# A two-layer hybrid transformer step: the loads of the first expert pairs, the last residual additions and the way of the outputs

## What is computed

```python
def layer(x, mod, P, l, ctx=None):
    h = rms_norm(x, P["norm_attn_pre"][l]) * (1 + sc1) + sh1
    a, new_ctx = token_mix(h, P, l, ctx)            # attention in three branches, gates, output projection
    x = x + g1 * rms_norm(a, P["norm_attn_post"][l])
    h = rms_norm(x, P["norm_ffn_pre"][l]) * (1 + sc2) + sh2
    x = x + g2 * rms_norm(moe(h, P, l), P["norm_ffn_post"][l])
    return x, new_ctx
```

## Time and profile before

| | us |
|---|---|
| median of 3 runs | 1754.84 (1752.04 to 1755.06) |
| the profiled execution | 1753.79 |
| its span, first to last instruction | 1752.0 |
| PE busy | 1679.8 (96%) |
| PEld, DVE, ACT, POOL busy | 900.7, 431.1, 321.6, 120.0 |
| share of PE in the chain that ended last | 91% |
| share of DMA in that chain | 4% |
| granted TensorE clock, mean | 0.986 of 2.4 GHz |
| moved by DMA | 559.88 MB |

### The profile page before, as it was taken

The page is one execution under the profiler, slowest core; times in us unless marked ns, Lnnn a source line. Parts: engine busy times, 40 slices in busy tenths (PEclk is TensorE's granted clock), DMA queues, the critical chain, the costliest instruction groups (busy, mean ns, idle before and its releaser), DMA issues.

```text
span 1752.0 us, 20948 instructions
## 1 busy us (share of the span) xinstructions
PE 1679.8 (96%) x8091; PEld 900.7 (51%) x8091; DVE 431.1 (25%) x1178; ACT 321.6 (18%) x754; POOL 120.0 (7%) x161
## 2 busy tenths in 40 slices
PE   4999998989999999999989999999899999999996
PEld 3878787643333333333367878784333333333332
DVE  1115443351111111111131444433311111111112
ACT  1010341021111111111120113302111111111111
POOL 3001000020000000001010000001100000000000
PEclk9999998999999999999999999899999999999998
DMA  9994232397999999999999633236879999999991
GB/s 354 418 388 161 88 105 70 139 363 302 367 424 426 426 424 425 425 426 425 418 394 404 226 109 105 85 108 253 341 288 414 426 425 425 425 423 425 426 426 80
DMA packets 60781, 559.88 MB, mean 320 GB/s; under 512 B 12972, under 2 KB 13120, under 8 KB 20240
## 3 DMA queue, kind: packets, MB, share of 16 engines
q1 hardware_dynamic: 45504, 528.50, 73.6%
q0 software_dynamic: 15184, 30.07, 5.0%
HBM read 576.02 MB, written 4.78 MB: 332 GB/s over the span
## 4 chain that ended last, share of the span: by engine, by line
PE 91%; DMA 4%; DVE 3%; issue 1%; ACT 1%; SPq 0%; POOL 0%; POOLq 0%; DVEq 0%; ACTq 0%; PEldq 0%
PE PS L1081 25%; PE PS L637 14%; PE PS L1109 13%; PE PS L1132 12%; PE PS L539 6%; PE PS L875 5%; PE PS L923 3%; DMA ring<-in_blocks 2%; PE PS L588 2%; PE PS L655 2%; PE PS L702 2%; PE PS L861 1%; DMA h_table<-region 1%; PE PS L765 1%; PE PS L820 1%
## 5 line engine op out<-in xcount | busy, mean ns | idle before, releaser
L1081 PE MATMUL PS<-ring,region 128*64 128x512 f32 x1920 | 425.6, 596 | 2.7 <-issue 1.5
L1081 PEld LDWEIGHTS PS<-ring,region 128*64 128x64 f32 x1920 | 138.8, 138 | 275.8 <-issue 275.7
L637 PE MATMUL PS<-region,ring 128*128 128x256 f32 x1088 | 245.2, 381 | 0.0
L1132 PE MATMUL PS<-region 128*128 128x512 f32 x512 | 241.0, 594 | 0.0
L637 PEld LDWEIGHTS PS<-region,ring 128*128 128x128 f32 x1088 | 203.8, 190 | 33.5 <-issue 6.3
L1109 PE MATMUL PS<-ring,region 128*64 128x512 f32 x960 | 219.2, 598 | 0.2
L1794 DVE SCALAR_TENSOR_TENSOR region<-region,PS 128x256 f32<-128x256 f32 x64 | 27.0, 421 | 673.4 <-ACT region L1363 673.4
L539 PEld LDWEIGHTS PS<-const,region 128*128 128x128 f32 (+1 forms) x925 | 106.9, 141 | 133.8 <-issue 75.7
L539 PE MATMUL PS<-const,region 128*128 128x128 f32 (+1 forms) x925 | 138.2, 279 | 31.4 <-DMA region<-in_c 11.9
L1109 PEld LDWEIGHTS PS<-ring,region 128*64 128x64 f32 x960 | 63.5, 136 | 147.5 <-issue 146.9
L1367 ACT ACTIVATE region<-PS 128x512 f32<-128x512 f32 x128 | 76.4, 597 | 265.7 <-PE PS L1109 265.7
(11 more groups left out here) (259 smaller groups left out, 1047.4 us busy)
## 6 DMA issues: line engine op xcount, KB each, us to landing
ring<-in_expert_blocks SPq DMA_DIRECT2D x180, 2048.0 KB, 16.2
ring<-in_blocks SPq DMA_DIRECT2D x120, 1024.0 KB, 17.4
region<-in_expert_blocks SPq DMA_DIRECT2D x8, 2048.0 KB, 16.3
region<-in_expert_blocks SPq DMA_DIRECT2D x8, 1024.0 KB, 16.4
region<-post_rows POOLq DMA_DIRECT2D x8, 512.0 KB, 8.3
h_table<-region POOLq DMA_DIRECT2D x4, 512.0 KB, 10.6
region<-in_w_kvk POOLq DMA_DIRECT2D x2, 640.0 KB, 14.0
region<-in_mla_w_ukv POOLq DMA_DIRECT2D x2, 512.0 KB, 18.0
```

What stands on the lines that cost most here:

```text
L637: last = pe.matmul(PS[:, j % 2, m * T:(m + 1) * T], w[:, k, m * P:(m + 1) * P], hT[:, k, :], start=(k == 0), stop=(k == KC - 1))
L1081: last = pe.matmul(PS[e * CAP:(e + 1) * CAP, 0, :], xe[:, k, e * CAP:(e + 1) * CAP], w[:, k % 4, :], start=(k == 0), stop=(k == KC - 1), s ...
L1132: last = pe.matmul(PS[:, 4 + 2 * t + half, :], hot[:, t * P:(t + 1) * P], og[:, half * HALF:(half + 1) * HALF], start=False, stop=True, sk ...
```

## The change

- `SPARE_PAIRS` and all that belongs to it is gone. All 32 pairs go through the ring, by one loop, and the three waits in SP's program ahead of the spare loads are gone with it. The small buffers of the router and the shared expert move to other places in `region`; they keep their sizes.
- After the second layer, tile 0's addition to `xr` is done by GpSimd. VectorE goes from the product of tile 0 straight to the root of tile 1.
- Tile 1's product and addition are done in two halves of 512 columns, each of which adds to `x_ready`.
- SP issues the outputs: `y_prompt` when GpSimd's addition is done, then each half of `y_sample`. SP waits for `y_out`; GpSimd's program ends with its addition.

```diff
-SPARE_PAIRS = (2, 17)
-PASS_ROUNDS = (EXPERT_LOADS - 6 * len(SPARE_PAIRS)) // RING_SLOTS
+PASS_ROUNDS = EXPERT_LOADS // RING_SLOTS
...
-                def experts_pass(base, q):
-
-                    for n in range(0, 8, 2):
-                        load_expert(n, n // 6, n % 6 // 2, base)
-                    sp.wait_ge(merged_ready, (l + 1) * KC)
-                    load_spare(SPARE_PAIRS[0], 0)
-                    sp.wait_ge(xn_tr, (l + 1) * 8)
-                    load_spare(SPARE_PAIRS[0], 1)
-                    load_expert(8, 1, 1, base)
-                    sp.wait_ge(state_out, (l + 1) * 6 * 16)
-                    sp.wait_ge(router_done, (l + 1) * 2)
-                    sp.wait_ge(shared_gu, (l + 1) * 2)
-                    load_spare(SPARE_PAIRS[0], 2)
-                    load_expert(10, 1, 2, base)
-                    load_pairs(3, 14, 12, base)
-                    sp.wait_ge(spare_used, sp.snap(q * 2) + 1)
-                    for part in range(3):
-                        load_spare(SPARE_PAIRS[1], part)
-                    load_pairs(18, 14, 8 * RING_SLOTS, base)
+                def experts_pass(base):
+                    with sp.Fori(0, PAIRS // 2) as i:
                         for u in range(2):
                             for part in range(3):
-                                load_expert(n + 6 * u + 2 * part, i * 2 + (first + u), part, base + i)
+                                load_expert(6 * u + 2 * part, i * 2 + u, part, base + i)
...
+            sp.wait_ge(last_ready, 1)
+            sp.dma_start(o["y_prompt"][0], xr[:, 0, :]).then_inc(y_out, 16)
+            for half in range(2):
+                cols = slice(half * HALF, (half + 1) * HALF)
+                sp.wait_ge(x_ready, DEPTH * 2 + half + 1)
+                sp.dma_start(o["y_sample"][0][:, cols], xr[:, 1, cols]).then_inc(y_out, 16)
+            sp.wait_ge(y_out, 48)
...
-            for t, name in enumerate(("y_prompt", "y_sample")):
-                pool.wait_ge(x_ready, DEPTH * 2 + t + 1)
-                apart(pool)
-                pool.dma_start(o[name][0], xr[:, t, :]).then_inc(y_out, 16)
-            pool.wait_ge(y_out, 32)
+            pool.wait_ge(last_scaled, 1)
+            pool.tensor_tensor(xr[:, 0, :], xr[:, 0, :], moe_scaled[:, 0, :], ALU.add).then_inc(last_ready, 1)
...
-                for t in range(2):
-                    add_normalised(6 + t, t, moe_scaled, 2, x_ready, EPS)
+                if l < DEPTH - 1:
+                    for t in range(2):
+                        add_normalised(6 + t, t, moe_scaled, 2, x_ready, EPS)
+                else:
+                    r = row_root(6)
+                    dve.wait_ge(postb_in, (l * 2 + 2) * 2 * 16)
+                    ve.scalar_tensor_tensor(out=moe_scaled[:, 0, :], in0=PS[:, 4:6, :].rearrange("p b n -> p (b n)"), scalar=r, in1=postb[:, 0, :],
+                                            op0=ALU.mult, op1=ALU.mult).then_inc(last_scaled, 1)
+                    r = row_root(7)
+                    for half in range(2):
+                        cols = slice(half * HALF, (half + 1) * HALF)
+                        step(ve.scalar_tensor_tensor(out=moe_scaled[:, 1, cols], in0=PS[:, 6 + half, :], scalar=r, in1=postb[:, 1, cols],
+                                                     op0=ALU.mult, op1=ALU.mult))
+                        ve.tensor_tensor(xr[:, 1, cols], xr[:, 1, cols], moe_scaled[:, 1, cols], ALU.add).then_inc(x_ready, 1)
```

85 lines of the change are left out of this document (26 added, 59 removed).

## The result

| five runs of each | median us | lowest to highest |
|---|---|---|
| before | 1755.06 | 1752.04 to 1758.82 |
| after | 1740.32 | 1737.41 to 1743.25 |

The ratio is 0.9906, with a 95% interval of 0.9881 to 0.9931: faster. It is worked out over all the runs, and the two medians alone stand 14.7 us apart, which is 0.9916. The median of after's own five runs, 1740.32, would have lain just inside it. The direction was right and the gain larger than expected. The profiled execution of after has a span of 1738.5 us (1752.0 before) at a granted clock of 0.991 (0.987).

What follows compares the result with a forecast made beforehand. TensorE was taken to bind the expert stages at 15.13 us a pair, with DMA nearly full. Gains of 1.5 (first layer), 4.0 (second) and 6.2 (end) summed to 11.7 us: 1743.1 us against the median 1754.84, range 1739.5 to 1750.0.

Steps and rivals of the forecast that it cites:

- the first layer gives 1.5 us: First layer's net gain: start earlier by 1.16 + 1.84 = 3.0 us, transfers later by 1.5.
- Start of the stage: Without spare loads the gather lands sooner and the lists bind; gate_up(0) starts 1.16 us and 2.16 us earlier.
- How the gather got its time: Table write and gather, 7.29 + 4.55 us, save some 1.2 us (first layer) and 2.2 (second); the write can give 4.4.
- The clock: The clock stays up over gate_up(0), which takes 6.87 us instead of 8.71: 1.84 us less in each layer.
- Pair 2 inside the stage: Its 14.8 us of loads fill 13.3 us of unused DMA time; transfers 1.5 us later, longest allowed wait 25.8 us.
- The boundary: Between the layers: the second layer starts when the transfers are through, not when TensorE is, costing 1.5 us.
- The end: GpSimd's drain no longer stands behind the outputs; outputs in at 1744.5, drain over at 1745.7: 6.2 us saved.
- The lock: Rival, 0.12: GpSimd's addition blocks tile 1's root on VectorE; last addition 2.3 us later, end saves 5.1, 1744.2 us.
- less 1.0 of scatter: Allowance for run scatter in the range's lower end, 1739.5 us.

Runs made afterwards that it cites:

- loads_only: Kernel before with only the loads and buffers of after (no spare buffers), its end unchanged: 1746.98 us, ratio 0.9963 to before.
- after_again: Kernel after, unchanged, measured a second time: 1738.39 us, ratio 0.9921 to before.
- after_third: Kernel after, unchanged, measured a third time: 1739.22 us, ratio 0.9915 to before.
- dve_adds: Kernel after with tile 0's last addition back on VectorE, none on GpSimd: 1740.65 us, ratio 0.9924 to before, tail 11.84 us.
- scalar_root: Kernel after with tile 1's last root in steps that read one SBUF tensor and scalars: 1740.34 us, ratio 0.9917 to before, tail 12.02 us.
- gpsimd_outputs: Kernel after with the three output transfers issued by GpSimd instead of SP: 1746.47 us, ratio 0.9957 to before, tail 18.77 us.
- shorter_end: Kernel after with tile 1's root by scalars and tile 0's product and GpSimd addition by halves: 1739.49 us, ratio 0.9925 to before.
- quiet_gather: Kernel after with pair 1's last two ring loads held back until the first gather landed: 1747.89 us, ratio 0.9966 to before.
- late_lists: Kernel after with a VectorE memset of about 2.1 us ahead of the lists' last max: 1747.46 us, ratio 0.9969 to before.
- before_look_2: Kernel before, unchanged, second of three single runs made for their traces: 1751.45 us.
- spare_late: Kernel before with both ring parts of pair 1 loaded first and pair 2's spare parts only after the first gather: 1758.09 us, ratio 1.0029.

## Why the prediction was wrong, point by point

The step that failed is the one behind "the first layer gives 1.5 us": that the second layer starts when the transfers are through, and that their 1.5 us are therefore taken off the first layer's gain. The transfers did come later, by 1.1 us. But 0.4 us of it was left 49 us behind the last gate_up and nothing at the end of the stretch, since VectorE's work on the residual takes as long as the transfers (the point on the boundary shows it). That is 1.5 of the 4.8 us by which the forecast was off. The other stretches together gave 0.1 us less than forecast, and the remaining 3.4 us are the subject of the last point.

The means of the six traces with early spare loads and of the eight of after's kind (loads_only, after, after_again, after_third, dve_adds, scalar_root, gpsimd_outputs, shorter_end), against the forecast. The tail is that of the kernels with the end of before, and with the end of after:

| stretch | with | without | difference | forecast |
|---|---|---|---|---|
| to stage 1 | 384.7 | 384.0 | -0.7 | 0 |
| start 1 | 475.77 | 472.31 | -3.5 | -3.0 |
| between | 379.6 | 379.6 | 0.0 | +1.5 |
| start 2 | 475.53 | 472.63 | -2.9 | -4.0 |
| tail | 18.56 | 12.58 | -6.0 | -6.2 |
| sum | | | -13.1 | -11.7 |

- **Start of the stage: right.** The gather left TensorE's path, the lists came next, as forecast. The gap shrank by 1.7 us in the first layer (4.37 to 2.65 in the mean; 1.16 forecast from a trace in which it was 3.87) and by 1.6 in the second (4.21 to 2.59; 2.16 forecast from 4.59). The gaps after the change were forecast at 2.71 and 2.43 us and came out at 2.65 and 2.59: what one trace gave wrong was each gap before, of which only the sum was typical.
- **How the gather got its time: half wrong.** The forecast let the write of the table give up to 4.4 us. The 512 KB write did fall (6.3 to 2.9 us), but the last write of the gates, which is the one in the chain, gave 0.8 us (7.29 to 6.52), and the gather itself 1.1 (4.55 to 3.48). The writes of the gates still stand behind a ring load of 2 MB, issued 0.8 us ahead of them (0.9 before). In the first layer that cost nothing, since the lists bind; in the second, quiet_gather's gap is 0.2 us shorter.
- **The clock: right in size, with the reason shown.** gate_up(0) took 7.09 us in all sixteen starts of the eight traces and 8.4 to 10 in eleven of the twelve others; late_lists brought the fall back with after's loads. In two second layers of after's kind (loads_only, dve_adds) it fell a little later, over down(0), at 1.3 us a time. The Trainium skill (TensorE: Matmul & The Clock Gate, section What's actually happening) says that the monitor runs freely, so that the same program can meet it at another phase, as the prediction cited. These traces agree: behind a gap of 3.86 us the clock stayed up in before_look_2, and behind one of 3.87 it fell in before.
- **Pair 2 inside the stage: right.** No stall; the longest wait of a load at the first stage's end, 23.5 to 24.2 us with the spare loads, is 24.1 to 26.1 without, 1.1 more in the mean, against 1.5 forecast and a limit of 25.8 that was, as it turns out, a little low.
- **The boundary: the step that failed.** "The second layer starts when the transfers are through" charged 1.5 us. The block that TensorE waits for does land 1.1 us later (24.7 us behind the start of the last gate_up in the mean of six, 25.8 of eight). But the first projection of the second layer (L655, after the change L623) needs more than the blocks: ScalarE's scaled inputs, which need VectorE's last small steps (L1510, L1450), and VectorE is busy nearly without a break with the end of the layer until then. That the earlier trace rows has the chain pass through the blocks is a close finish: in before TensorE's transposes behind them ended at 891.18, VectorE's step at 891.16. First before, then after_again, whose last gate_up starts at 859.81 and 857.67 us (timelines of PE and DVE):

```profile
884.35 3.66 PE L588 MATMUL PS<-ring,condT 128*32 128x256 f32 x64 [2.52 <-DMA ring<-in_blocks]
...
890.99 0.17 DVE L1510 SCALAR_TENSOR_TENSOR pre<-modT,parT 128x16 f32<-128x16 f32 x1
...
893.20 7.11 PE L655 MATMUL PS<-region,ring 128*128 128x256 f32 x24 [2.02 <-ACT region L1200]
```
```profile
882.93 3.66 PE L556 MATMUL PS<-ring,condT 128*32 128x256 f32 x64 [3.24 <-DMA ring<-in_blocks]
...
888.84 0.17 DVE L1450 SCALAR_TENSOR_TENSOR pre<-modT,parT 128x16 f32<-128x16 f32 x1
...
891.05 9.30 PE L623 MATMUL PS<-region,ring 128*128 128x256 f32 x42 [1.28 <-ACT region L1140]
```

  TensorE's wait for the block ends 24.5 us behind the last gate_up in the one and 25.3 in the other, VectorE's step stands at 31.2 in both, and the projection starts at 33.4 in both.

  In seven of the fourteen traces it starts at 33.4, with blocks landing from 24.4 to 25.1; in gpsimd_outputs, with 25.7, at 33.6. The six others start at 34.6 to 36.6, and in each of them the clock was low over the matmuls on that block (5.35 us in after, 3.66 above): five of the eight without spare loads, one of the six with them. Three of those with spare loads have a low stretch just behind instead, over the projection.

  At TensorE's next matmuls of that kind, 48.4 and 48.9 us behind the last gate_up in the means, 0.4 us of the delay is left, and over the whole stretch "between" nothing. The stretch also differs within one and the same kernel by where the clock was low: in after for 3.4 us from 882.2 and for 10.2 from 1121.2 (382.1 us in all), in after_again for 3.4 from 1127.2 alone (377.4). With that last pattern the kernels with the spare loads take 377.2 and 377.3 us, those without them 377.3, 377.4 and 377.5.
- **The end: right in sum, by luck.** The lock, a rival with 0.12, was real and cost 2.0 us (dve_adds: 0.7 back, net of an addition of 1.24). The halves landed in 2.0 us, not 2.9, so the outputs were in 1.1 us later than forecast. The forecast had them in 1.3 us ahead of the end, which that took up; GpSimd's drain, which I had as the end, was over just before the last landing (1737.7 against 1738.1). GpSimd's addition took 2.34 us (2.65 taken; the estimate of 2.3 from the Trainium skill, GPSIMD Engine Reference, section Elementwise — side-by-side cycle accounting, was closer).
- **The range: too narrow at its lower end.** It allowed for the 1.5 us of the boundary; what it had too small is "less 1.0 of scatter", from three runs that lay within 3 us. Over 101 runs the kernel before spreads by 16.6 us, and medians of groups of it lay from 1752.1 to 1755.1. The first comparison's own interval is 4.4 us wide on either side. Of the 4.8 us between forecast and result, 2.4 are of this kind (16.5 by the first ratio, 14.1 over all runs), 1.4 are terms (13.1 against 11.7: 1.5 at the boundary, and 0.7 before the first expert stage, where the forecast had no term and the low stretch of the clock near 270 us differs from trace to trace, less 0.8 by which the two starts and the end fell short), and 1.0 is between the traces' sum and the runs. All the sums, 11.7 among them, lie within the runs' 11.1 to 15.9. Whether the last 2 us belong to the change or to chance stays open.

## What to carry to other kernels

Look, for each large prefetch, at which small transfer it meets and who waits for that one: here 2 MB beside two writes of 32 KB cost 4.6 us, 8 MB ahead of a gather 5.4, and moving the loads moved the harm with them. A wait of some 4 us ahead of dense matmuls cost more than itself here, since the clock fell behind it. Where two paths end close together, as the blocks and VectorE's steps do at the boundary, a delay of one of them may cost nothing: look how late the other is before charging it. At a program's end, ask what still has to drain behind the last transfer, and issue that transfer from an engine that has little to drain. And take the scatter of a range from many runs, not from three, above all where a stretch that the change does not touch varies by more than the change.

## What the runs showed of the chip that I had not expected

- GpSimd's last drain took 5.54 or 5.62 us where it began when the last transfer had landed (before, loads_only, spare_late, gpsimd_outputs), and it ended 5.4 us behind GpSimd's last addition in the seven kernels that end with one. In dve_adds, where it has nothing to do at the end, its drain began at 1675.3, took 12.8 us, and was over long before.
- A GpSimd addition over 1024 columns held a VectorE instruction of one column for 2.0 us, and not at all once that read one tensor instead of two.
- A write of 32 KB in rows of 256 bytes landed in 1.7 us alone and in 6.0 to 8.6 beside 2 MB loads.
- Behind a gap of 3.7 to 5.0 us the granted clock fell to its lower level (1.2 of 2.4 GHz) over gate_up(0) in thirteen of fourteen starts; behind 2.4 to 2.9 us in none of twenty-two.
